# Attention steps every three and a half weight slabs, convolution shares moved one block earlier, gate sigmoids cut into pairs

## The reference, cut to what matters

```python
h = rmsnorm(x, g_pre_mix)
q, k, v, glu_a, glu_b, gate_sb, gate_cv = split(h @ w_in + b_in)      # w_in: 2048 x 9216
# stick-breaking attention, 8 heads of 128, over query blocks of 128
z = (q @ k.T) * scale
log_1m = where(mask, log_sigmoid(-z), 0)
suffix = reverse_cumsum(log_1m) - log_1m
o_sb = where(mask, exp(log_sigmoid(z) + suffix), 0) @ v @ w_sb_out
# the convolution branch
u = glu_a * sigmoid(glu_b)
u = silu(layernorm(causal_depthwise_conv(u, w_dw, b_dw)))             # 31 taps, 1024 channels
o_cv = u @ w_conv_out
merged = sigmoid(gate_sb) * o_sb + sigmoid(gate_cv) * o_cv
y = merged @ w_o
```

## Time and profile before

| | us |
|---|---|
| median of 3 runs (lowest, highest) | 3098.55 (3097.56, 3099.07) |
| the profiled execution's own time | 3098.79 |
| its span in the trace | 3097.0 |
| TensorE matmuls busy | 2885.4 (93%) |
| VectorE busy | 1971.7 (64%) |
| ScalarE busy | 1446.5 (47%) |
| GpSimd busy | 74.0 (2%) |

### The profile page before, as it was taken

How to read it: one execution, slowest core, us unless ns; L and a number is a source line. 1 busy time by engine, 2 the same in 40 slices (tenths; PEclk the granted TensorE clock), 3 DMA queues, 4 the chain that set the end, 5 groups by cost and what they waited for, 6 DMA issues and landing times.

```text
span 3097.0 us, 51788 instructions
## 1 busy us (share of the span) xinstructions
PE 2885.4 (93%) x19568; PEld 2514.7 (81%) x19568; DVE 1971.7 (64%) x2513; ACT 1446.5 (47%) x1866; POOL 74.0 (2%) x90
## 2 busy tenths in 40 slices
PE   6999999979999999997998996887968999999997
PEld 5888888868888888886877885776856888888886
DVE  4588886656556565657865566546657656565665
ACT  4445656554444444445476335325435444444443
POOL 0000000010000000010000000000102000000001
PEclk9999999989999999998999997999988999999999
DMA  5655554636565666653644341013624666666664
GB/s 173 184 186 173 168 172 136 202 114 183 188 186 189 186 190 188 188 186 108 190 155 132 116 123 41 3 43 95 197 75 149 187 188 188 189 186 190 185 192 132
DMA packets 480985, 484.50 MB, mean 156 GB/s; under 512 B 14736, under 2 KB 479632, under 8 KB 480704
## 3 DMA queue, kind: packets, MB, share of 16 engines
q1 hardware_dynamic: 480288, 479.01, 50.0%
q0 software_dynamic: 544, 3.38, 0.3%
HBM read 480.23 MB, written 2.10 MB: 156 GB/s over the span
## 4 chain that ended last, share of the span: by engine, by line
PE 43%; DVE 6%; ACT 3%; issue 1%; POOL 0%; DMA 0%; ACTq 0%; POOLq 0%; DVEq 0%; SPq 0%
PE pg L375 24%; PE pg L382 12%; DVE lo L312 1%; PE p L783 1%; PE p L797 1%; PE p L800 1%; PE p L1156 1%; DVE rw_xx L849 0%; ACT hi L276 0%; PE p L459 0%; POOL sq_sum L440 0%; DVE half L487 0%; DVE dnc L884 0%; PE p L1397 0%; DVE resid L331 0%
## 5 line engine op out<-in xcount | busy, mean ns | idle before, releaser
L312 DVE TENSOR_TENSOR lo<-raw,hi 128x1024 fp32r<-128x1024 f32 x904 | 1100.2, 1231 | 818.4 <-ACT hi L276 814.5
L276 ACT ACTIVATE hi<-raw 128x1024 fp32r<-128x1024 f32 x904 | 947.2, 1058 | 1165.5 <-PE pg L382 1160.3
L375 PE MATMUL pg<-xa,hi 128*128 128x512 f32 x4608 | 1174.7, 397 | 38.7 <-DVE xa L476 37.0
L375 PEld LDWEIGHTS pg<-xa,hi 128*128 128x128 f32 x4608 | 835.9, 190 | 198.9 <-issue 44.4
L375 PE MATMUL pg<-xb,hi 128*128 128x512 f32 x2624 | 664.7, 395 | 10.6 <-DVE xb L579 2.9
L382 PEld LDWEIGHTS pg<-xa,lo 128*128 128x128 f32 x4608 | 631.4, 191 | 46.0
L382 PE MATMUL pg<-xa,lo 128*128 128x256 f32 x4608 | 644.5, 283 | 0.0
L375 PEld LDWEIGHTS pg<-xb,hi 128*128 128x128 f32 x2624 | 475.7, 190 | 99.0 <-ACT hi L276 4.4
L382 PEld LDWEIGHTS pg<-xb,lo 128*128 128x128 f32 x2624 | 358.8, 191 | 28.3 <-DVE lo L312 2.4
L382 PE MATMUL pg<-xb,lo 128*128 128x256 f32 x2624 | 366.7, 283 | 2.0 <-DVE lo L312 2.0
L286 ACT ACTIVATE half<-pg 128x512 f32<-128x512 f32 x212 | 123.7, 583 | 83.8 <-PE pg L382 83.8
(11 more groups left out here) (364 smaller groups left out, 1649.8 us busy)
## 6 DMA issues: line engine op xcount, KB each, us to landing
raw<-w_in SPq DMA_DIRECT2D x264, 512.0 KB, 4.6
raw<-ffn_w SPq DMA_DIRECT2D x256, 512.0 KB, 4.0
raw<-w_up SPq DMA_DIRECT2D x128, 512.0 KB, 3.9
raw<-w_down SPq DMA_DIRECT2D x128, 512.0 KB, 4.4
raw<-w_o SPq DMA_DIRECT2D x32, 512.0 KB, 4.5
raw<-w_out SPq DMA_DIRECT2D x32, 512.0 KB, 3.5
raw<-w_sb_out SPq DMA_DIRECT2D x16, 512.0 KB, 4.7
raw<-w_conv_out SPq DMA_DIRECT2D x16, 512.0 KB, 4.7
```

The lines of the kernel that those rows point to most:

```text
L276: nc.scalar.activation(hi[:, slot], raw[:, slot], ACT.Copy).then_inc(hi_ready, 1)
L312: nc.vector.tensor_tensor(lo[:, slot], raw[:, slot], hi[:, slot].bitcast(F32), ALU.subtract).then_inc(lo_ready, 1)
L375: nc.tensor.matmul(pg[:, par, t, :], lhsT=hi[:, slot, k, c:c + P], rhs=g.x[:, kk, :], start=(j == 0 and k == 0), stop=False)
```

## The change

Three edits, all in the first block's mixer.

1. The attention steps are called by the hook `each`, on all three engines, in place of `after(m)`: step i at hook 3 + 7i // 2, so at hooks 3, 6, 10, 13, 17, 20, 24, 27, 31, 34, 38, 41, 45, 48, 52, 55 and 59 of the 64 slabs. From an even step to the odd one it is three slabs, from an odd step to the even one four. The seventeenth step, formerly behind slab 63, follows slab 59.
2. The convolution: nine steps to each of the 8 blocks of `g_gsb`, eight to each of the first 7 of `g_gcv`, none to the last. It stays in `after(m)`.
3. The gates' sigmoids: sixteen of two tiles each. Pair m + 1 is made behind the taking of block m of the projection that uses it, pair 0 ahead of the projection, and VectorE waits for the pair in `evacuate`.

```diff
@@ evacuate
             own = g.sum0 + t + 1
+            if g.kind == "mult":
+                dve.wait_ge(gates_done, (0 if g is g_sbo else 8) + t + 1)
@@
         def share(m):
-            a0 = 10 * m if m < 12 else 120 + 8 * (m - 12)
-            return conv_steps[a0:a0 + (10 if m < 12 else 8)]
+            a0 = 10 * m if m < 12 else 120 + 9 * (m - 12) if m < 20 else 192 + 8 * (m - 20)
+            return conv_steps[a0:a0 + (10 if m < 12 else 9 if m < 20 else 8)]
+
+        ATT_HOOKS = [3 + 7 * i // 2 for i in range(2 * SB_H + 1)]
+
+        def att_steps(eng, step):
+            for hook in range(4 * (g_gsb.blocks + g_gcv.blocks)):
+                if hook in ATT_HOOKS:
+                    step(eng, ATT_HOOKS.index(hook))
+                yield
@@
+        def gate_act(act, tile0, m):
+            if m < 8:
+                nc.scalar.activation(pair(gates(tile0), m), pair(gates(tile0), m), ACT.Sigmoid).then_inc(gates_done, 1)
@@ scalar
-            gemm_act(act, g_gsb, lambda m: att_act(act, m), follows=g_gcv)
-            gemm_act(act, g_gcv, lambda m: att_act(act, m + 8), follows=g_sbo)
-            att_act(act, 16)
+            att = att_steps(act, att_act)
+            gemm_act(act, g_gsb, follows=g_gcv, each=step_of(att))
+            gemm_act(act, g_gcv, follows=g_sbo, each=step_of(att))
             blocks_out(act, g_gcv)
-            nc.scalar.activation(gates(TGS), gates(TGS), ACT.Sigmoid).then_inc(gates_done, 1)
-            nc.scalar.activation(gates(TGC), gates(TGC), ACT.Sigmoid).then_inc(gates_done, 1)
-            gemm_act(act, g_sbo, lambda m: ln_act(act, m), follows=g_cvo)
-            gemm_act(act, g_cvo, lambda m: merge_act(act, m - 1), follows=g_wo)
+            gate_act(act, TGS, 0)
+
+            def sbo_beside(m):
+                gate_act(act, TGS, m + 1)
+                ln_act(act, m)
+            gemm_act(act, g_sbo, sbo_beside, follows=g_cvo)
+            gate_act(act, TGC, 0)
+
+            def cvo_beside(m):
+                gate_act(act, TGC, m + 1)
+                merge_act(act, m - 1)
+            gemm_act(act, g_cvo, cvo_beside, follows=g_wo)
@@ vector
-            def beside(m):
-                att_dve(dve, m)
-                conv(dve, share(12 + m))
-            gemm_dve(dve, g_gsb, beside, follows=g_gcv)
-            gemm_dve(dve, g_gcv, lambda m: beside(m + 8), follows=g_sbo)
-            att_dve(dve, 16)
-            dve.wait_ge(gates_done, 2)
+            att = att_steps(dve, att_dve)
+            gemm_dve(dve, g_gsb, lambda m: conv(dve, share(12 + m)), follows=g_gcv, each=step_of(att))
+            gemm_dve(dve, g_gcv, lambda m: conv(dve, share(20 + m)), follows=g_sbo, each=step_of(att))
@@ tensor
-            gemm_pe(pe, g_gsb, lambda m: att_pe(pe, m))
-            gemm_pe(pe, g_gcv, lambda m: att_pe(pe, m + 8))
-            att_pe(pe, 16)
+            att = att_steps(pe, att_pe)
+            gemm_pe(pe, g_gsb, each=step_of(att))
+            gemm_pe(pe, g_gcv, each=step_of(att))
             pe.wait_ge(att_lo, SB_H)
```

## The result

The change makes the kernel slower. The changed kernel took 3106.99 us (median of 11 runs, 3104.24 to 3109.75), the kernel before, on the same chip, 3097.56 us (11 runs, 3096.16 to 3099.07). The ratio is 1.0031 with a 95% interval of 1.0021 to 1.0040, that is, 9.6 us more with 6.5 to 12.4. The forecast was 3113.0 us in a range of 3102 to 3119. The profiled execution took 3106.49 us, with a span of 3104.7 us against 3097.0 before. All comparisons are between fast runs; one slow run (6889.5 us, of the kernel with gate pairs alone) is in none of them.

The account below looks back on a forecast made before the run. TensorE was taken to be full in most of the kernel, with VectorE having little to spare beside the attention. -8.3 + 0.6 + 19.1 + 2.8 = +14.2 us on 3098.79 gave 3113.0 us, range 3102 to 3119.

Parts of the forecast that it names:

- Then VectorE sets the pace: Attention stage: from even step 2 on, VectorE's work sets the time, putting head 7's masked scores (`att_sp`) at 454.8.
- The end of the stage: From slab 63 to slab 2 of the output projection: 10.5 us replaces 18.86, -8.3 us.
- The steps between slabs: Attention stage: VectorE late at even steps, TensorE waits behind slabs 13, 20, 27, 41, 48 and 55; +19.1 us.
- TensorE's clock: Slow clock behind TensorE's waits, counted behind the last and by about half behind slab 27; +2.8 us, bounds 0 and 5.
- The gates in pairs: Output projection: gate pair 4 ahead of the normalisation's eight sigmoids lengthens TensorE's 1.50 us wait for `hi`; +0.6 us.
- The steps are met in time: Attention stage: VectorE early enough at even steps, stage keeps its length, both gaps vanish; 3091.1 us, chance 0.08.
- The two cancel: Attention stage: VectorE's waits for `hi` behind odd steps are hidden, stage loss 9.5; 3100.6 to 3103.4 us, chance 0.09.
- A vicious circle: Attention stage: slow clock behind each of six waits delays `hi` and with it VectorE; 3121.6 us, chance 0.05.

Follow-up runs that it names:

- the kernel with the old shares: The changed kernel, but with eight convolution taps to each of the 16 gate blocks; ratio 1.0017 to the kernel before.
- the pairs early: The changed kernel with taps in VectorE's waits, and gate pairs 2, 3 and 4 made one or two blocks earlier; ratio 0.9967 to the kernel before.
- the fastest version: The changed kernel with five taps in each even step's Ln wait, three behind each odd step, five after each block until done; 3086.89 us.
- the other spacing: The changed kernel with four slabs from an even step to its odd one, three from odd to even; ratio 1.0024 to the kernel before.

## Why the prediction was right, and where not

**The direction and the mechanism** were right. *"Then VectorE sets the pace"* is shown from both sides: taking eight taps out of its way brings the last mask 4.9 us forward, filling its waits gives all of the loss back, and changing the spacing without changing its work gives 2.2 us of 9.6.

**The end of the stage, -8.3 us.** 8.85 us where there were 18.86, of which the two steps' matmuls are paid elsewhere: 0.90 (455.14 to 456.04) and 0.6. That makes -8.5. Right, but the account of the second gap was not: the taps of the last share were part of it.

**The steps between slabs, +19.1 us.** Head 7's mask let TensorE go at 455.14; forecast 454.8. Behind slab 55 an unhindered TensorE would have been at 435.7, so it lost 19.4 us, 0.5 of which stood ahead of the stage. The first wait was to last 3.0 us and took 2.73. The total and the places of the six are right. What the forecast had wrong is how TensorE loses the time: it expected about 19 us of waiting, and the waits make 12.5.

**TensorE's clock, +2.8 us.** This is the term that was mis-sized. Most of the 6.9 us that the waits leave open is TensorE at a lower clock: behind the waits that end at 307.32, 359.02 and 430.36 the step and its slab took 5.4 us each, behind the other three 3.8, which makes 4.7 together. But since VectorE sets the pace, a slow slab mostly shortens the next wait. It could count in full behind the last wait alone, and that one was 0.95 us long, not 3, because the slab behind the wait before it had been slow, and it left no slow slab: the four slabs behind it took 11.27 us (456.04 to 467.31). In the kernel with the old shares the fifth wait left no slow slab, the last one was 2.52 us, and the slab behind it was slow; there the term would have counted. By half it was to count behind slab 27, and there 0.73 us did go through: VectorE waited so long for `hi` at 374.14, which it did not where that slab ran at full clock. But the sum for VectorE already had about 1 us for this place. So the term added nothing to the 19.4. The forecast said that it is hidden where the next step waits, and yet took the last wait at 3 us.

**The gates in pairs, +0.6 us.** The wait ahead of slab 10 went from 1.50 to 2.02 us, and with the pairs early to 1.51: right. In this execution another thing covered it. TensorE's timeline of the changed kernel:

```profile
516.23 3.64 PE L377 MATMUL pg<-xb,hi 128*128 128x512 f32 x8 [2.02 <-ACT hi L276]
...
525.90 1.22 PE L384 MATMUL pg<-xb,lo 128*128 128x256 f32 x8 [0.46 <-DVE lo L312]
```

The slow clock came behind the wait for `hi`, which made the following wait for `lo` 0.46 instead of 2.02. In the trace before it came behind the wait for `lo`, 3.46 us for eight matmuls. From slab 2 to the next projection it took 47.33 us against 48.34. The gates alone showed no difference in time.

**The sum.** At slab 2 the changed kernel is 10.9 us late (forecast, without the gates: 13.6), at the next projection 9.9 and at the end of the span 7.7. In the stages behind, whose instructions are the same, the two executions drift by 2.2 us; the runs say 9.6 (6.5 to 12.4). Without the clock term the forecast would have been +11.4.

**Rivals.** *The steps are met in time* is what the changed kernel does when VectorE has half the taps or has them in its waits; the forecast's 3091.1 for it compares with 3087.8 and 3086.9 us. In the fastest version slab 2 of the projection starts at 468.89 (465.62 and 3.27 for the sums), 8.2 us before its time in the kernel before: the 8.3 of the forecast. What the runs show beyond it, up to 10.5 (6.8 to 14.3), lies behind that point and within the interval. *The two cancel* stood on the waits for `hi` being hidden: they aren't, 1.54 us each, and without them the time is 3094.7. *A vicious circle* didn't form: but for the 0.73 us behind slab 27, the clock's losses were absorbed.

## What to carry to other kernels

Before dealing steps out more finely, follow one of them through all its engines: when does each queue reach it, and what does the queue that arrives first hold back meanwhile. An engine that is busy for 79% of a stretch can be the one that sets the pace, if the rest are waits inside its own chain. Independent work put into those waits (here five taps ahead of the Ln, three behind the exponent) gained 20 us, the other spacing 2. A mean that agrees with a forecast says little when the runs lie in two groups; then the trace has to show the step. An edit that is worth nothing alone, as the gate pairs, can be worth 6 to 8 us once the gap that covered the old form is closed.

## What the runs showed of the hardware that was not expected

The same wait doesn't cost the same in clock. (Each kernel has one traced execution.) The wait of 2.02 us for `hi` ahead of slab 10 of the output projection stood in eight kernels in the same place. Behind it the eight high matmuls took 3.64 us in the changed kernel, 3.13 with taps behind odd steps, 3.06 with half the taps, and 2.08 or 2.09 in the five others. So the loss is between 0 and 1.6 us for one and the same gap. This agrees with what the forecast cited from the Trainium skill (TensorE: Matmul & The Clock Gate, Part 1), that the activity count isn't aligned to the kernel's work. Since the following wait for `lo` hangs on ScalarE and VectorE and not on TensorE, the slow slab was taken back there in each of the three cases (0.46, 0.45 and 0.48 us of wait instead of 2.02).
